# A decoder layer on one core: the direction in which TensorE reads its moving operand and writes PSUM

## The reference

```python
h = _rms_norm(x, attn_norm_g[l])
proj = h @ w_in[l]
...
merged = (jax.nn.sigmoid(g_da) * (o_da @ w_o_da[l])
          + jax.nn.sigmoid(g_ret) * (o_ret @ w_o_ret[l])
          + jax.nn.sigmoid(g_mem) * (o_mem @ w_o_mem[l]))
x = x + merged @ w_out[l]
hf = _rms_norm(x, ffn_norm_g[l])
x = x + (jax.nn.silu(hf @ w_ffn_gate[l]) * (hf @ w_ffn_up[l])) @ w_ffn_down[l]
```

## Time and profile before

| what | value |
|---|---|
| median of 2 runs | 1627.88 us (1627.53 and 1628.24) |
| span of the profiled execution | 1625.4 us |
| what lies around the span in an execution | 2.1 to 2.8 us, so the profiled execution's own time is 1627.5 to 1628.2 us |
| PE busy | 1618.2 us, 100% of the span |
| PEld busy | 1339.3 us, 82% |
| DVE busy | 1271.1 us, 78% |
| ACT busy | 908.2 us, 56% |
| DMA | 341 MB, mean 210 GB/s |

### The profile page before, as it was taken

The page is one execution under the profiler, slowest core; times in us unless marked ns, Lnnn a source line. Parts: engine busy times, 40 slices in busy tenths (PEclk is TensorE's granted clock), DMA queues, the critical chain, the costliest instruction groups (busy, mean ns, idle before and its releaser), DMA issues.

```text
span 1625.4 us, 20227 instructions
## 1 busy us (share of the span) xinstructions
PE 1618.2 (100%) x7373; PEld 1339.3 (82%) x7373; DVE 1271.1 (78%) x1325; ACT 908.2 (56%) x989; POOL 80.6 (5%) x73
## 2 busy tenths in 40 slices
PE   9999999999999999999999999999999999999999
PEld 7888888888888888888888888888888888888887
DVE  5565545589777777777975589999999999999995
ACT  6654454555555554445554465656655665656653
POOL 0000000000011100000000000100100100100101
PEclk9999999999999999999999999999999999999999
DMA  9876555556554555566675756868868868868866
GB/s 339 278 214 194 157 180 175 174 179 220 179 166 162 164 172 168 174 188 199 202 245 182 249 166 207 252 211 248 246 212 250 249 208 249 244 220 240 253 211 178
DMA packets 178007, 341.35 MB, mean 210 GB/s; under 512 B 11793, under 2 KB 16401, under 8 KB 177169
## 3 DMA queue, kind: packets, MB, share of 16 engines
q1 hardware_dynamic: 167056, 319.45, 60.4%
q0 software_dynamic: 10880, 20.97, 7.1%
HBM read 317.31 MB, written 2.10 MB: 197 GB/s over the span
## 4 chain that ended last, share of the span: by engine, by line
PE 90%; issue 6%; DVE 1%; DMA 1%; POOL 1%; ACT 1%; SPq 0%; DVEq 0%; ACTq 0%; POOLq 0%
PE acc L1582 43%; PE at L1664 9%; PE at L1666 9%; PE at L1665 9%; PE acc L1666 5%; PE acc L1664 5%; PE acc L1665 5%; PE at L1582 3%; PE at L1604 2%; POOL rstd L480 1%; PE at L1642 0%; PE at L1657 0%; DMA raw<-in_w_mem_kv 0%; DMA raw<-in_w_in 0%; DVE w_lo L929 0%
## 5 line engine op out<-in xcount | busy, mean ns | idle before, releaser
L929 DVE TENSOR_TENSOR w_lo<-raw,w_hi 128x1024 fp32r<-128x1024 f32 x319 | 386.6, 1222 | 239.6 <-ACT w_hi L507 235.4
L507 ACT ACTIVATE w_hi<-raw 128x1024 fp32r<-128x1024 f32 x319 | 337.1, 1060 | 360.9 <-PE acc L1582 300.3
L1582 PE MATMUL acc<-w_hi,hT_hi 128*128 128x512 f32 x752 | 297.6, 396 | 0.0
L1582 PE MATMUL acc<-w_hi,hT_lo 128*128 128x512 f32 x752 | 293.1, 390 | 0.0
L1582 PE MATMUL acc<-w_lo,hT_hi 128*128 128x512 f32 x752 | 293.0, 390 | 0.0
L857 ACT ACTIVATE f_hi<-sum 128x2048 fp32r<-128x2048 f32 x60 | 115.3, 1922 | 121.2 <-DVE sum L1461 118.0
L1582 PEld LDWEIGHTS acc<-w_hi,hT_hi 128*128 128x128 f32 x752 | 141.2, 188 | 30.9 <-issue 1.3
L1582 PEld LDWEIGHTS acc<-w_hi,hT_lo 128*128 128x128 f32 x752 | 141.2, 188 | 29.7
L1582 PEld LDWEIGHTS acc<-w_lo,hT_hi 128*128 128x128 f32 x752 | 141.3, 188 | 28.4
L1582 PE MATMUL acc<-w_hi,oT_hi 128*128 128x512 f32 x384 | 151.2, 394 | 1.5 <-DVE oT_lo L955 1.4
L1582 PE MATMUL acc<-w_hi,oT_lo 128*128 128x512 f32 x384 | 149.6, 390 | 0.0
(11 more groups left out here) (349 smaller groups left out, 2658.1 us busy)
## 6 DMA issues: line engine op xcount, KB each, us to landing
raw<-in_w_in SPq DMA_DIRECT2D x208, 512.0 KB, 3.8
f_raw<-in_w_ffn_down SPq DMA_DIRECT2D x88, 512.0 KB, 4.8
f_raw<-in_w_ffn_gate SPq DMA_DIRECT2D x80, 512.0 KB, 3.9
f_raw<-in_w_ffn_up SPq DMA_DIRECT2D x80, 512.0 KB, 5.0
proj<-down POOLq DMA_DIRECT2D x40, 512.0 KB, 6.4
raw<-in_w_mem_kv SPq DMA_DIRECT2D x32, 512.0 KB, 6.2
raw<-in_w_out SPq DMA_DIRECT2D x32, 512.0 KB, 3.7
raw<-in_w_o_mem SPq DMA_DIRECT2D x16, 512.0 KB, 5.0
```

The source lines that it names most:

```text
L507: act.activation(w_hi[:, s % RING], raw[:, s % RING], ACT.Copy).then_inc(hi_done, 1)
L929: v.tensor_tensor(w_lo[:, s % RING], raw[:, s % RING], w_hi[:, s % RING].bitcast(F32), ALU.subtract).then_inc(lo_done, 1)
L1582: e = pe.matmul(dst, a[:, k0 + k, tok], w[:, s % RING, k, :], start=first and k == 0 and n == 0, stop=last and k == 1 and n == 2)
```

## The change

Both helpers now give the matmul its moving operand and its destination with the columns in reverse, each with a step of -1: column 511 of the weights is streamed first and column 511 of the PSUM bank is written first, column 0 last. The same weight column still meets the same result column, so all addresses hold the same numbers afterwards. The stationary operand keeps its order. Transposes and the small float32 matmuls keep theirs too. No instruction is added, removed or moved, on any engine; the order of TensorE's instructions is the same row by row, but for the line numbers of `product`, which is one line longer.

```diff
@@ -1579,7 +1579,7 @@
                 for n, (a, w) in enumerate(((hi, w_hi), (hi, w_lo), (lo, w_hi))):
-                    e = pe.matmul(dst, a[:, k0 + k, tok], w[:, s % RING, k, :],
+                    e = pe.matmul(dst[:, ::-1], a[:, k0 + k, tok], w[:, s % RING, k, ::-1],
                                   start=first and k == 0 and n == 0, stop=last and k == 1 and n == 2)
@@ -1661,6 +1661,7 @@
             def product(dst, hi, lo, whi, wlo, first, last):
 
+                dst, whi, wlo = dst[:, ::-1], whi[:, ::-1], wlo[:, ::-1]
                 pe.matmul(dst, hi, whi, start=first, stop=False)
```

## The result

The changed kernel takes 1668.16 us (1667.98 to 1668.34) against 1627.88 us: a ratio of 1.0249, 95% interval 1.0233 to 1.0266. It is slower by 40.3 us. That lies inside the stated range (1612 to 1720 us) and outside my forecast of no change, to which I had given a chance of 0.71.

What follows compares the result with a forecast made beforehand. TensorE was taken as the bound, matmul count times pitch. Zero for read, write and fixed part left the span at 1625.4 us; with 2.1 to 2.8 us around it, forecast 1628 us, own range 1615 to 1645, stated range 1612 to 1720.

Steps and rivals of the forecast that it cites:

- forecast of no change: Whole kernel: reversing the columns leaves the time at 1628 us, own range 1615 to 1645 us; chance 0.71.
- The frame: Whole kernel: TensorE's pitch sets the time; 6789 of 7373 matmuls are touched, 6789 x 226.9 ns = 1540 us.
- rival C: Each reversed matmul pays some cycles more at its start, 13.6 ns; 92 us more, 1720 us; chance 0.08.
- I take 0 for all three: The 6789 matmuls: backward read, backward PSUM write and the fixed part per matmul each change the pitch by 0.
- The third term: Per matmul: 13.6 ns above the columns, likelier tied to the stationary operand; change 0, bounds -13.6 to +13.6 ns.
- hidden: Stationary operand's load: 188 ns inside a pitch of 226.9 ns, so it stays hidden at that pitch.
- decision point of 4.8 ns: Per reversed matmul: 4.8 ns more makes 32.6 us, 2% of the kernel, enough to count as slower.
- B: Reversed matmuls run at half rate, two cycles a column; 1392 us more, 3020 us; chance 0.16.
- D: The fixed 13.6 ns per reversed matmul vanishes; 92 us less, 1536 us, floor around 1540 us; chance 0.05.

Runs made afterwards that it cites:

- e8: Kernel before, moving operand and destination reordered: L1582 in falling pairs, product in falling runs of 16 columns, each rising; 1669.46 us.
- e12: Kernel before, L1582's stationary operand shifted with a forward moving operand, or alone with a backward one; product swaps neighbouring columns; 1637.39 us.
- e2: Kernel before with only the PSUM destination written backward, moving operand read forward; 1627.35 us, ratio 0.9997.
- e11: Kernel before with only L1582's stationary operand begun 2 to 128 columns off its place; 1638.59 us.
- e4: Kernel before, each matmul but a group's first split into two of 256 columns, both backward, upper half first; 1690.4 us against 1710.1 for forward halves.
- e5: Kernel before with directions mixed: L1582's second pass backward, product's first two passes backward and third forward; 1653.84 us, ratio 1.0162.
- e6: Kernel before, moving operand and destination in blocks of 128 columns: L1582 falling blocks, each rising; product rising blocks, each reversed; 1646.85 us.
- e9: Kernel before, L1582's moving operand read forward from other start columns (2 to 512); product in falling runs of 64, each rising; 1637.07 us.
- e10: Kernel before, L1582's moving operand read backward from start columns 511 to 1023, PSUM forward; product in falling runs of 32, each rising; 1669.21 us.
- e3: Kernel before, each matmul but a group's first split into two forward ones of 256 columns; 1710.1 us.

## Why the prediction was right and wrong

**The frame was right.** TensorE's pitch sets the time, the diff touches 6789 matmuls, nothing else moves, and the sum is a count times a difference in pitch. The kernel after shows all of it: the same waits but for 0.2 us, same clock, same costs of the small matmuls, DVE at 76%. Three readings of rows were off and changed nothing in the sum. The stationary operand doesn't change with each matmul: it is loaded for each, but the passes hi x w_hi and hi x w_lo use the same one. The float32 rate of the earlier trace rows is two cycles a column for a record, and a float32 matmul leaves two records (L1657 is reached 16 times and has 32), so the whole matmul takes four. And the runs that list both numbers have 1.7 to 1.8 us around the span, not 2.1 to 2.8 (here 1668.34 and 1666.6).

**The range was met by luck.** The forecast's own range, 1615 to 1645 us, was missed. The stated one holds 1668.16 us only because rival C's 1720 us was added to it, at a chance of 0.08, with a size and reasons that didn't come true.

**The step that failed is "I take 0 for all three", and in it the read.** I argued that the matmuls stay nearest to the rows of their own kind because adjacent elements stay adjacent. Adjacency isn't what counts: pairs in falling order (e8) pay the full price, swapped neighbours in rising order (e12) none. Of the three terms the moving operand took 6.4 ns where I put 0 between bounds of 0 and 205 ns, PSUM took 0 (e2).

**The third term is where the price sits.** I called the 13.6 ns "fixed per matmul", said that they were more likely tied to the stationary operand, and concluded from it that the direction would leave them alone, because the load of 188 ns is hidden in the pitch. What the runs support of the first half is that the stationary operand takes part in what stands above the columns: shifting it alone brings up to 6.6 ns (e11, 8 columns), and shifting both by 8 to 48 columns takes that away (e12). The conclusion failed: the direction didn't leave the part above the columns alone, it went from 32 cycles to 48. And "hidden" was no argument: in e11 the load is as before but for its address, and the matmul takes longer. That the backward price comes from the same meeting of two reads is likely but only argued: the halves of e4 and the neighbours in e5 speak for it, and no shift took it away.

**Rival C came closest, with the wrong size and the wrong mechanism.** It asked for some cycles more per stream and took one more 13.6 ns, 92 us, 1720 us, at a chance of 0.08. It was 6.4 ns, about half of that, 43 us. Its test, a pitch between 232 and 241 ns on all four lines and small matmuls as before, is what the profile shows. But its reasons, an address to be formed or a line met from its odd end, fall with the halves of e4, which don't pay, and with the start at column 1 in e12, which doesn't either. The decision point of 4.8 ns a matmul was right, and 6.4 is just over it.

**B and D.** No half rate anywhere: with 512 columns the highest mean of any stage is 235.9 ns. The Trainium skill's sentence on non-contiguous patterns ("PSUM — Partial Sum Buffer", "Specifications (TRN2)") is not borne out for these orders: e2 writes PSUM backward at a ratio of 0.9997, and falling blocks of 128 (e6) and swapped pairs (e12) are written at 226.7 ns. The Trainium skill's sentence on 16-byte lines ("SBUF — State Buffer", "Door 1: The DMA port swizzle") doesn't describe the price of 6.7 ns: falling pairs and runs of 16 keep such lines and pay it, and from runs of 64 columns (256 bytes) on it is gone. Nothing gave back any of the 32 cycles at 512 columns, so D has no support; only the backward halves of e4 went below 32, to 28, in a kernel that is slower for having twice the matmuls.

**What stays open.** That a forward matmul's time depends on where the moving and the stationary operand begin relative to each other, with a period of 256 bytes, is what e9, e11 and e12 show by their times. Which part of the chip they share, why a falling order never finds a cheap position, and why 16 cycles is the usual step, they don't show. A backward load of the stationary operand wasn't tried, and the position was never swept finely for the backward stream; that no shift helps is shown for seven of the stationary operand (e12) and for thirteen starts of the stream (e10). No version here beats the kernel before: the tiles of its large matmuls all begin at the same place modulo 256 bytes, and are read in rising order, which is the cheapest combination found.

## What to carry to other kernels

When TensorE is the bound, read its cost as the distance between starts, in cycles, and ask what stands above the number of columns: here 32 of 544 and later 48 of 560, on thousands of matmuls. Keep both operands of a float32r matmul in step: rising order, and starts that leave the same remainder at 256 bytes; a view two or 32 columns into a tile (233.4, and 232.3 to 233.3 ns) costs nearly as much as a backward one. "It is hidden" bounds an operation's own time, not what it does to the operation that hides it.

## What the runs showed of the hardware

- Writing PSUM from the last column to the first is free: 1627.35 against 1628.05 us, ratio 0.9997 (0.9988 to 1.0007).
- Reading the moving operand backward costs 16 cycles for 512 columns (544 to 560), and not for 256 (288 to 284).
- A forward matmul of 512 float32r columns takes 226.7 ns where moving and stationary operand begin at the same remainder of 64 columns, and mostly 229 to 233 ns where they don't; exceptions are a stationary operand 4 columns off (227.4 ns) and both 2 columns off (231.2 ns).
- A backward matmul of 512 columns takes 233.3 to 233.5 ns from the last of a group of four columns (seven starts), and 235.6 to 235.9 ns from the first or second of one (six starts).
- Weight loads overlap each other: 191 ns each, one every 120 ns (e3).
- Neighbours swapped in rising pairs cost nothing (226.7 ns), and neither do falling runs of 64 or 128 columns; falling runs of 2, 16 and 32 cost 6.7, 6.7 and 5.8 ns (moving operand and destination reordered together).
